# Two chunks' key products ahead of the last pooled input tile, and the second chunk's substitution right behind the first

## The reference, cut to what matters

```
h = concat(meta, x)                                   # 1040 x 1024
proj = rms_norm(h) @ w_in
qkv, z, b, a, pool_in, gates = split(proj)
q, k, v = split(silu(causal_conv(qkv)))               # 8 heads of 128
o = chunk_gated_delta_rule(l2(q), l2(k), v, g, beta)
y_b = (windowed_mean(pool_in) - pool_in) @ w_pool     # 4 windows: 2, 4, 8, 16
y = sigmoid(g_a) * norm(o) * silu(z) + sigmoid(g_b) * y_b
h = h + y @ w_out
h = h + conv_gated_mlp(rms_norm(h))
```

```
lower = where(strict, einsum('hncd,hnsd->hncs', kb, k) * decay, 0)
tinv  = triangular_solve(lower + eye, eye)
u, w  = tinv @ (v * beta), tinv @ (kb * exp(g))
```

## Time and profile before

| what | value |
|---|---|
| median of 3 runs | 1717.13 us (1716.76 to 1719.14) |
| the profiled execution: its own time | 1718.44 us |
| its span, first to last instruction | 1716.6 us |
| TensorE busy | 1675.1 us, 98% of the span |
| TensorE weight loads | 1603.8 us, 93% |
| DVE, ACT, POOL busy | 896.9, 600.3, 494.5 us |
| mean granted TensorE clock | 0.994 of full |

### The profile page before, as it was taken

How to read it: one execution, slowest core, us unless ns; L and a number is a source line. 1 busy time by engine, 2 the same in 40 slices (tenths; PEclk the granted TensorE clock), 3 DMA queues, 4 the chain that set the end, 5 groups by cost and what they waited for, 6 DMA issues and landing times.

```text
span 1716.6 us, 30495 instructions
## 1 busy us (share of the span) xinstructions
PE 1675.1 (98%) x12103; PEld 1603.8 (93%) x12103; DVE 896.9 (52%) x969; ACT 600.3 (35%) x982; POOL 494.5 (29%) x473
## 2 busy tenths in 40 slices
PE   7999999998999999999899999999999999999997
PEld 6999999998899999999899998998998998989986
DVE  5556454574444545444542665544545446455447
ACT  6333465544443434434333431221221211212214
POOL 3212212255445344453221132121212211221210
PEclk9999999999999999999999999999999999999999
DMA  5222443358555464554883121111111111211112
GB/s 182 71 93 97 131 147 90 92 157 142 149 167 140 119 158 114 141 163 109 208 270 97 38 62 50 37 49 49 49 37 39 59 49 37 61 48 38 49 37 98
DMA packets 242511, 168.23 MB, mean 98 GB/s; under 512 B 43913, under 2 KB 228840, under 8 KB 241306
## 3 DMA queue, kind: packets, MB, share of 16 engines
q1 hardware_dynamic: 209494, 135.30, 28.4%
q10 hardware_dynamic: 32740, 32.08, 5.6%
q0 software_dynamic: 224, 0.12, 0.0%
HBM read 125.10 MB, written 42.37 MB: 98 GB/s over the span
## 4 chain that ended last, share of the span: by engine, by line
PE 90%; DVE 3%; issue 2%; POOL 1%; POOLq 1%; ACT 1%; DMA 1%; DVEq 0%; ACTq 0%; SPq 0%
PE gb L878 66%; PE db L1224 11%; PE db L1022 4%; PE mb L1224 2%; PE db L936 1%; POOL w_lo L761 1%; PE db L1093 1%; PE db L1092 1%; DVE cacc L1735 1%; POOLq L810 1%; DMA yo<-ot_d 1%; POOLq L807 1%; DVE fino L2153 0%; PE db L1019 0%; PE db L1164 0%
## 5 line engine op out<-in xcount | busy, mean ns | idle before, releaser
L878 PE MATMUL gb<-u_hi,w_hi 128*128 128x342 f32 (+2 forms) x2520 | 821.9, 326 | 8.6 <-DVE u_lo L2021 5.1
L878 PE MATMUL gb<-u_lo,w_hi 128*128 128x342 f32 (+2 forms) x2520 | 809.5, 321 | 0.0
L878 PE MATMUL gb<-u_hi,w_lo 128*128 128x342 f32 (+2 forms) x2520 | 806.8, 320 | 0.0
L761 POOL TENSOR_TENSOR w_lo<-w_raw,w_hi 128x1024 fp32r<-128x1024 f32 x130 | 327.9, 2526 | 1048.8 <-ACT w_hi L1268 1048.7
L878 PEld LDWEIGHTS gb<-u_hi,w_hi 128*128 128x128 f32 x2520 | 477.4, 189 | 12.9 <-issue 9.2
L878 PEld LDWEIGHTS gb<-u_lo,w_hi 128*128 128x128 f32 x2520 | 477.6, 190 | 0.4
L878 PEld LDWEIGHTS gb<-u_hi,w_lo 128*128 128x128 f32 x2520 | 477.1, 189 | 0.0
L1268 ACT ACTIVATE w_hi<-w_raw 128x1024 fp32r<-128x1024 f32 x130 | 135.6, 1052 | 5.5 <-ACT tm L1367 5.2
L1735 DVE SCALAR_TENSOR_TENSOR cacc<-xb,prm,cacc 128x1040 f32<-128x1040 f32 x72 | 124.6, 1731 | 10.4 <-issue 8.4
L2118 DVE TENSOR_TENSOR h<-h,db 128x512 f32<-128x512 f32 x138 | 92.5, 684 | 42.2 <-PE db L1224 41.8
L1634 ACT ACTIVATE a_hi<-cv 128x1024 fp32r<-128x1024 f32 x21 | 22.3, 1060 | 248.8 <-PE db L1224 200.5
(11 more groups left out here) (264 smaller groups left out, 1824.0 us busy)
## 6 DMA issues: line engine op xcount, KB each, us to landing
w_raw<-in_w_in SPq DMA_DIRECT2D x53, 512.0 KB, 4.2
w_raw<-in_w_up SPq DMA_DIRECT2D x44, 512.0 KB, 3.8
w_raw<-in_w_down SPq DMA_DIRECT2D x22, 512.0 KB, 3.5
qkT_d<-sl ACTq DMA_DIRECT2D x16, 576.0 KB, 2.8
kv_d<-tm ACTq DMA_DIRECT2D x16, 576.0 KB, 3.4
tk<-kv_d SPq DMA_DIRECT2D x9, 1024.0 KB, 7.6
w_raw<-in_w_out SPq DMA_DIRECT2D x11, 512.0 KB, 8.6
kT<-qkT_d SPq DMA_DIRECT2D x9, 512.0 KB, 5.0
```

The costliest lines, as they stand in the source:

```text
L761: pool.tensor_tensor(lo, w_raw[:, n % SLOTS, :], hi.bitcast(F32), ALU.subtract).then_inc(s_wlo, 1)
L878: mm = pe.matmul(gb[:, bank, 0:w], wt, u, start=(k == 0 and m == 0), stop=(k == KT - 1 and m == 2))
```

## The change

The key product of chunk 1 (`("KK", 1)`) and the query product of chunk 0 are done before pooled input tile 3; the step `KK` of pass 0 is gone. SP stores the blocks of chunk 1 ahead of `blocks_back(0)` and loads them back inside it, with `store_pooled(2)` behind; 3 and 4 follow, then `load_qT(1)`, then 5 to 7. POOL runs `substitute(1)` right behind `substitute(0)`, with two `w_low`, `values_part(0)` and `keys_part(0)` inside it after rounds 2, 5, 8 and 11 (counted from 0); `tth`, the column of `gs` and the third `w_low` come after it. `rr` is cleared by DVE in `first_inverse`. ACT's third `w_high` moves up to behind product 4. SP's third weight load of pass 0 moves behind the loads of chunk 2. POOL's pass 0 is written out ahead of its loop.

```diff
-POOL_PLAN = [("tile", 1, (0,)), ("KK",), ("tile", 1, (1, 2)), ("tile", 2, (0, 1, 2)), ("pool", 0), ("pool", 1),
-             ("tile", 3, (0, 1, 2)), ("QK",)] + [("pool", j) for j in range(2, KT)]
+POOL_PLAN = [("tile", 1, (0,)), ("KK", 0), ("tile", 1, (1, 2)), ("tile", 2, (0, 1, 2)), ("pool", 0), ("pool", 1),
+             ("QK", 0), ("KK", 1), ("tile", 3, (0, 1, 2))] + [("pool", j) for j in range(2, KT)]
@@ SP
-            def blocks_out(c):
+            def blocks_stored(c):
                 sp.wait_ge(s_ev["KK"], 2 * c + 2)
                 for p in range(P // SQ):
                     sp.dma_start(by_rows(blk_d)[square(p)], at_m[square(p), :, square(p)]).then_inc(s_bst, 16)
+
+            def blocks_loaded(c):
                 sp.wait_ge(s_bst, 16 * (P // SQ) * (c + 1))
                 for e in range(2):
                     sp.dma_start(sub_rows(blk, e), sub_blocks(blk_d, e)).then_inc(s_blk, 16)
...
-                if not first(c):
+                if first(c):
+                    blocks_loaded(1)
+                    store_pooled(2)
+                else:
                     sp.wait_ge(s_rd, c)
                 sp.wait_ge(s_sst, 32 * c + 32)
...
             load_tk(0)
+            sp.wait_ge(s_blk, 32)
+            blocks_stored(1)
             blocks_back(0)
+            for j in range(3, 5):
+                store_pooled(j)
             sp.wait_ge(s_ps["QK"], 2)
             load_qT(1)
-            for j in range(2, KT):
+            for j in range(5, KT):
                 store_pooled(j)
...
-                blocks_out(i + 1)
+                if not first(i):
+                    blocks_out(i + 1)
                 for j, c0 in enumerate((Z_COL, GA_COL, GB_COL)):
-                    load_w(W_ZG + 3 + j, cols(w_in, c0 + P + P * i), i)
+                    if not first(i) or j < 2:
+                        load_w(W_ZG + 3 + j, cols(w_in, c0 + P + P * i), i)
...
                 chunk_loads(i + 1, False)
+                if first(i):
+                    load_w(W_ZG + 5, cols(w_in, GB_COL + P))
@@ POOL
                     if first(c) and j == 3:
                         w_low(W_POOL + 4)
+                    if second(c):
+                        if j == 2:
+                            w_low(W_ZG)
+                        elif j == 5:
+                            pool.wait_ge(s_tk, 16)
+                            pool.wait_ge(s_ev["QK"], 2)
+                            values_part(0)
+                        elif j == 8:
+                            w_low(W_ZG + 1)
+                        elif j == 11:
+                            pool.wait_ge(s_g, U_ZG)
+                            keys_part(0)
...
             substitute(0)
-            for j in range(3):
-                w_low(W_ZG + j)
-            pool.wait_ge(s_tk, 16)
-            pool.wait_ge(s_ev["QK"], 2)
-            values_part(0)
-            pool.wait_ge(s_g, U_ZG)
-            pool.memset(rr[:, :, :], 0.0).then_inc(s_zero, 1)
+            pool.wait_ge(s_sst, 32)
+            substitute(1)
             pool.memset(tth[:, :, :], 0.0)
             pool.memset(gs[:, 0:1], 0.0).then_inc(s_yg, 16)
-            keys_part(0)
-            pool.wait_ge(s_sst, 32)
+            w_low(W_ZG + 2)
@@ ACT
             for j in range(2, KT):
                 scale_pool(j)
-            w_high(W_ZG + 2)
+                if j == 4:
+                    w_high(W_ZG + 2)
@@ DVE
                     dve.wait_ge(s_dec, c + 1)
+                    if second(c):
+                        dve.wait_ge(s_bst, 16 * (P // SQ))
...
-                elif q == 3:
+                elif q == 2:
                     dve_step("QK", 0)
+                    dve_step("KK", 1)
...
             def first_inverse():
+                dve.wait_ge(s_g, U_ZG)
+                dve.memset(rr[:, :, :], 0.0)
+                drain()
                 dve.wait_ge(s_bd, 16)
-                dve.wait_ge(s_zero, 5)
```

More of the change, by code:

```diff
@@ L451, in hybrid_block, with second @@
         s_out = [sem(f"s_out{i}") for i in range(OUT_SLOTS)]
+        def second(n):
+            return isinstance(n, int) and n == 1
         def gain(row, n=KT):
@@ L571, in blocks_out @@
                     sp.dma_start(sub_rows(blk, e), sub_blocks(blk_d, e)).then_inc(s_blk, 16)
+            def blocks_out(c):
+                blocks_stored(c)
+                blocks_loaded(c)
             def blocks_back(c):
@@ L824, in _ @@
             substitute(0)
-            for j in range(3):
-                w_low(W_ZG + j)
-            pool.wait_ge(s_tk, 16)
-            pool.wait_ge(s_ev["QK"], 2)
-            values_part(0)
-            pool.wait_ge(s_g, U_ZG)
-            pool.memset(rr[:, :, :], 0.0).then_inc(s_zero, 1)
+            pool.wait_ge(s_sst, 32)
+            substitute(1)
             pool.memset(tth[:, :, :], 0.0)
             pool.memset(gs[:, 0:1], 0.0).then_inc(s_yg, 16)
-            keys_part(0)
-            pool.wait_ge(s_sst, 32)
+            w_low(W_ZG + 2)
             def chunk(i, last):
-                substitute(i + 1)
+                if not first(i):
+                    substitute(i + 1)
                 if not last:
@@ L850, in chunk @@
                     w_low(W_ZG + 3 + j, i)
-            with pool.Fori(0, HEADS - 1) as i:
+            chunk(0, False)
+            with pool.Fori(1, HEADS - 1) as i:
                 chunk(i, False)
@@ L1114, in _ @@
                 else:
+                    c = item[0]
                     pe.wait_ge(s_tm, QKV_TILES)
-                    step(kind, 0, None)
+                    step(kind, c, (kind, 0) if c else None)
             def piece(p, i):
@@ L1143, in chunk @@
                         freed = (held[-1], 2 * i if held[-1] in DOUBLING else 2 * i + 2)
-                    if not (name == "P1" and first(c)):
+                    if not (name in ("KK", "P1") and first(i)):
                         step(name, c, (LAST_Y, 0) if freed[0] == "P1" and first(c) else freed)
@@ L1981, in chunk @@
                         decayed_keys(1)
-                    else:
+                    elif not (name == "KK" and first(i)):
                         dve_step(name, i if name in REC else i + 1)
```

## The result

The changed kernel takes 1707.92 us (median of 7 runs, 1703.53 to 1709.51) against 1716.76 for the kernel before beside it (7 runs): ratio 0.9947, 95% interval 0.9937 to 0.9956, faster by 0.53%. The forecast was 1706.6, in a range of 1703.2 to 1711.5. The profiled execution took 1707.96 with a span of 1706.1, against 1716.6 before.

The account below looks back on a forecast made before the run. TensorE, busy 98% of the span, was taken as the bound, so only its gaps could give time. Terms of 0.9 + 5.1 + 4.5 = 10.5 us off 1717.1 gave 1706.6 us, range 1703.2 to 1711.5.

Parts of the forecast that it names:

- gap B: TensorE's 3.42 us wait before 420.45, step `V` of chunk 0 waiting for `rr`; removal was to give 5.1 us.
- slow clock: TensorE at clock 0.50 (1.2 GHz) for about 3.4 us after a gap, losing 1.7 us each time.
- gap C: TensorE's 2.81 us wait before 448.23, step `X0` of chunk 1 waiting for `rrs`; removal was to give 4.5 us.
- Gap A: TensorE's 3.42 us wait before 404.82, product 6 waiting for `p_lo`; this part was to give 0.9 us.
- the price of the short gap: A gap of about 2 us before pass 0's first unit was charged 1.7 us of slow clock, bounds 0 and 1.7.
- The stores: With `qT` moved behind store 4, store 2 lands at 404.7, store 3 at 408.5; pass 0's first unit starts at 409.0.
- from chunk 2 on nothing is to be won by earlier results: TensorE was busy for all 52.40 us of a later pass, so no gain was expected there.
- The port: Rival, 11%: POOL's moved `w_low` gets in before DVE's last subtraction, `p_lo` comes 2.4 to 3 later; 1709.5 us.
- The queue: Rival, 11%: chunk 1's `sol` stands behind three large loads, `X0` waits 2 to 4 us plus slow clock; 1711 us.
- No price for the short gap: Rival, 17%: store 3 lands nearer 407.5, or the clock stays at 2.4 GHz; 1704 us.
- No change: Rival, 4%: chunk 1's blocks land late, POOL starts at 411, `V` waits for `vb`; 1.5 us gained, 1715.5 us.
- slower: Rival, 3%: `V` waits on a late substitution; a start at 415 eats the gain, 418.5 gives 1720.6 us.

Follow-up runs that it names:

- e1_again: The changed kernel, run again without any edit: 1708.9 us, ratio 0.9935 to the kernel before.
- e12_again: The changed kernel, run once more without any edit on another chip: 1707.24 us, ratio 0.9929 to the kernel before.
- e4_qt_first: The changed kernel with `load_qT(1)` ahead of store 2 again: 1708.27 us, ratio 0.9938 to the kernel before.
- e5_port: The changed kernel with POOL's first moved `w_low` one round earlier: 1705.84 us, ratio 0.9916 to the kernel before.
- e6_bds_late: The changed kernel with store 3 ahead of the `bds` load of chunk 0: 1706.64 us, ratio 0.9922 to the kernel before.
- e7_rr_pool: The changed kernel with `rr` cleared by POOL again, behind `vb` inside the second substitution: 1706.91 us, ratio 0.9923 to the kernel before.
- e10_yl_behind: e5_port with the wait for all stores and the load of `yl` behind `bds` of chunk 1: 1706.37 us, ratio 0.9926 to the kernel before.
- e9_half_stores: The changed kernel with stores of products 2 to 7 halved, half the pooled output left out: 1704.6 us, ratio 0.9919 to the kernel before.
- e3_outside: The changed kernel with two `w_low` ahead of the second substitution, `vb` and `kd` behind it, none inside: 1711.98 us, ratio 0.9954 to the kernel before.
- e8_before: The kernel before, measured against itself: 1718.53 us, ratio 0.9995.
- e2_b_alone: The kernel before with only `rr` cleared by DVE and `vb` ahead of POOL's third `w_low`: 1718.04 us, ratio 0.9992.
- e11_both: e10_yl_behind with the edit of e6_bds_late and a wait for chunk 0's `bds` ahead of storing chunk 1's `sol`: 1706.33 us, ratio 0.9926.

## Why the prediction was right

**The total** came out 1.3 us above the forecast, with two errors that nearly cancel: that the sum below fits to a tenth is luck. By the medians the change gained 8.8 us (1716.76 less 1707.92) where 10.5 were forecast, and 10.5 and 12.4 in e1_again and e12_again. Step by step, in the profile of the change:

| part | forecast | measured | how |
|---|---|---|---|
| up to the first unit | 0.9 | 3.4 | 411.61 - 407.94, less 0.25 of offset |
| first unit to `V` (gap B) | 3.4 | 3.6 | 8.84 before, 5.27 now |
| `V` to `X0` (B's slow clock, gap C) | 4.5 | 4.6 | 27.78 before, 23.22 now |
| `X0` to `KK` of the loop (C's slow clock) | 1.7 | 1.4 | 20.15 before, 18.70 now |
| behind it | 0 | -2.5 | 13.0 less 10.5 of span |
| sum | 10.5 | 10.5 | |

**Gap A: the price of the short gap was the step that failed.** The mechanism held: POOL's two `w_low` gone from beside line 1935, 1.25 us for 5.91, `p_lo` at 403.34 (forecast 403.5), product 6 at 403.50 (403.6), and then the stores decide. The first unit starts about 0.7 us after store 3 has landed, in every profile in which ACT waits for it (407.2 and 407.94 in the change, 408.1 and 408.77 in e1_again, 407.8 and 408.48 in e4_qt_first, 407.5 and 408.16 in e5_port, 406.8 and 407.51 in e6_bds_late, 408.0 and 408.74 in e7_rr_pool, 407.6 and 408.36 in e10_yl_behind, 408.0 and 408.71 in e12_again), and in e9_half_stores, where it had landed 3 us before, right behind product 7. The sum had store 3 at 408.5 and 1.7 us for a slow clock. It landed at 407.2, and no slow clock followed. Of the 2.5 us by which the term was short, 1.7 is the clock and the rest the store. e1_again and e4_qt_first, with half clock there, have `KK` of the loop at 457.48 and 457.19 (forecast 458), the profiles with whole stores, without it and without a late `vb` or `bds`, at 455.13 to 455.92. So the bounds of 0 and 1.7 were right, and the chip goes now one way, now the other.

**The stores.** I took it that moving the load of `qT` away from ahead of store 2 mattered. With the load back there (e4_qt_first) nothing is lost that can be told from chance, since `QK` is done early and `qT` is issued 1.6 us ahead of store 2; its old distance of 0.6 us was not tried in the new order. The forecast of 5.3 us for store 2 was 0.8 too long.

**Gap B.** Right, with its cover: `rr` was ready at 409.7 (409.8 forecast), `vb` at 410.5 (409.9 to 411), `V` came at 413.2. Clearing `rr` on DVE took 0.91 us, inside the bounds of 0.9 to 1.3. e7_rr_pool and e3_outside show the two sides of the cover: `rr` ready at 413.7, 4 us later, is free, `vb` at 418.4 is not.

**Gap C.** Right. `sol` stood behind `yl` and `tk` as forecast, `bds` landed at 431.2 instead of 436.2 because the last store landed at 421.1, not 424.3. `X0` had about 4.5 us of cover in this profile (`rrs` is made 0.6 after `bds`), 2.3 in e12_again, where the last store landed at 424.2, 0.7 in e7_rr_pool and none in e6_bds_late. So the part is right, and its cover is thin in some executions.

**Two errors of sight.** The first: "from chunk 2 on nothing is to be won by earlier results" was taken to mean that nothing could be lost there either. TensorE's idle time between `KK` of the loop and the last pass's `P1` is 0 to 0.2 us in the three profiles that have the old order (before, e8_before, e2_b_alone). In the eleven with the new order it is 0.2 to 2.5, with a median of 1.4: at one step of pass 1 near 494, and near 813 and 820. All are called "issue". In the profile of the change the one near 494 stands in the middle of a step's matmuls, between two that read the same tiles. That the new order gives some of its gain back here, 1.4 us in the median, is what the profiles show; why is not shown. The second: the gap at 863.16 was 1.82 and is 3.61 here. In the other two profiles of the changed kernel it is 1.80 (e1_again) and 1.41 (e12_again). The longer gap by itself costs little: from the unit at 835.88 to that at 863.16 it is 27.28 us, before (847.45 to 874.50) 27.05, since the half clock that stood behind 847.45 is missing now and TensorE comes to the same wait earlier. What costs about 1 us is the half clock of 6.8 us around the gap instead of 3.4 behind it; this part is taken for chance.

**The rivals.** *The port* did not come in the change: POOL's `w_low` started at 403.60, 0.26 after `p_lo` was done. One round earlier it is a race (e5_port lost by POOL, e10_yl_behind and e11_both won by it). The mechanism is as the rival had it, but its price is not: I wrote that product 6 and the clock would bring 1709.5. The profiled executions of e10_yl_behind and e11_both, with `p_lo` 2.0 late, took 1706.48 and 1707.51, where that of e12_again, on the same chip and with `p_lo` in time, took 1707.05: no half clock followed, and the store ends last or nearly so. The Trainium skill, "SBUF — State Buffer", section "SBUF: two separate sides", says that the pair of ports is locked for a whole instruction by whoever starts first; the four rows of e5_port and e10_yl_behind agree, 3.34 for POOL's 2.40 in one and 3.25 for DVE's 1.24 in the other. But who was first can't be read from the recorded starts to a tenth: in the earlier trace rows DVE is recorded 0.06 us ahead and still waited for both of POOL's operations. *The queue* came in the profile of e6_bds_late at 1.81 us plus a slow clock. *No price for the short gap* is what the profile of the change shows up to the loop: it would have given 1704, and the profile's 455.13 is on that course until the later gaps take 2.5 back. *No change* and *slower* needed a substitution that starts at 411, and at 415 or later; it started at 398.78 (I had 400.0), and nothing of them was seen. What e2_b_alone adds is that the 5.1 us of gap B and the 4.5 of gap C are not two gains that can be had one by one.

## What to carry to other kernels

When several gaps in a hand-over hang on one chain, find its last link first: mending gap B alone (e2_b_alone) moved the same microseconds to the next. Place a large elementwise operation on POOL by what DVE does in those microseconds, not only by when its result is due: one round earlier than in the changed kernel, DVE won the race once and POOL twice. Behind each gap that is closed, ask which transfer ends next; here that was a store's landing, and it hid a `p_lo` that was 2.0 us late, down to the last 0.30 us (e10_yl_behind).

## What the runs showed of the hardware

- **A gap of about 2 us may or may not be followed by half clock.** Ahead of the first unit: 1.28, 1.59, 1.94 and 2.18 us not followed, 2.17 and 2.61 followed; ahead of product 6, 2.56 (e10_yl_behind), 2.55 (e11_both) and 2.65 (e3_outside) not followed, where the kernel before had it after 3.42 and 3.27. At one and the same unit of the output phase, 1.82 was followed (before) and 1.80 was not (e1_again). Even the 3.30 ahead of 835.88 was not followed in the profile of the change, and was in e1_again and e12_again. What else decides was not found.
- **The port goes to one of the two, and the loser's duration in the trace contains its wait.** DVE 0.17 us ahead won (e5_port), POOL 0.63 ahead won (e10_yl_behind, e11_both), but DVE 0.06 ahead lost.
- **Stores that run together landed in the order of their issue**, 2.5 to 4.2 us apart for 513 KB in the profile of the change (403.6, 407.2, 409.7, 413.9, 417.1, 421.1), up to 6.5 apart in e11_both and e12_again. A small DMA mostly landed when the store issued just ahead of it did: `bds` of chunk 0 at 403.8, 0.2 behind store 2 (2.3 behind in e1_again); in the kernel before, the first of chunk 1's blocks at 424.2, 11.5 us after its issue, about when the last store landed (424.4).
- **Clearing 128x1024 floats took DVE 0.91 us** (at 406.94), POOL 0.96 (e7_rr_pool).
